# GpSimd's modulation slots through buffers and a queue of their own

## What is computed

```python
c_act = silu(c)
for layer in range(2):
    mod = c_act @ mod_w[layer] + mod_b[layer]
    sh1, sc1, g1, sh2, sc2, g2 = split(mod, 6)
    u = rms_norm(h, norm_mix[layer]) * (1 + sc1) + sh1
    mix = hgrn2_mixer(u, ...) if layer == 0 else chunk_band_attention(u, k_pad, v_pad, ...)
    h = h + g1 * mix
    u = rms_norm(h, norm_ffn[layer]) * (1 + sc2) + sh2
    h = h + g2 * swiglu(u, ffn_w_in[layer], ffn_w_out[layer])
    if layer == 0:
        k_pad, v_pad = shared_kv(h, c_act, kv_norm, kv_mod_w, kv_mod_b, kv_w)
```

## Time and profile before

| | |
|---|---|
| median of 3 runs | 2322.44 us (2321.78 to 2323.91) |
| the profiled execution | 2321.61 us |
| its span, first to last instruction | 2319.6 us |
| mean granted TensorE clock | 0.975 |
| TensorE busy | 2189.9 us (94%) |
| VectorE, ScalarE, GpSimd busy | 1410.4, 752.1, 424.3 us |
| GpSimd's multiply L593, 36 times | 3690 ns mean |
| GpSimd's first add L594, 36 times | 3473 ns mean |
| loads on SP into `raw` | 218 of 1024 KB, 4.8 us to landing |

### The profile page before, as it was taken

The page is one execution under the profiler, slowest core; times in us unless marked ns, Lnnn a source line. Parts: engine busy times, 40 slices in busy tenths (PEclk is TensorE's granted clock), DMA queues, the critical chain, the costliest instruction groups (busy, mean ns, idle before and its releaser), DMA issues.

```text
span 2319.6 us, 25720 instructions
## 1 busy us (share of the span) xinstructions
PE 2189.9 (94%) x10094; PEld 1752.1 (76%) x10094; DVE 1410.4 (61%) x1929; ACT 752.1 (32%) x961; POOL 424.3 (18%) x272
## 2 busy tenths in 40 slices
PE   7899999979999997999989999998999998999997
PEld 5588788767888886866678888876568876888885
DVE  5666766554767767177455444467565776655656
ACT  1443334332222223256432222244233333322321
POOL 0000000039998873200000000000420000000000
PEclk9999999989999998999999999999999998999998
DMA  6343231225555542422122322322112221323220
GB/s 245 124 161 109 92 127 57 71 84 188 200 182 182 182 163 94 143 91 74 52 76 91 99 101 91 109 94 69 41 48 98 92 81 65 109 91 109 91 91 37
DMA packets 39327, 249.54 MB, mean 108 GB/s; under 512 B 4627, under 2 KB 4819, under 8 KB 11112
## 3 DMA queue, kind: packets, MB, share of 16 engines
q1 hardware_dynamic: 32856, 230.97, 28.7%
q0 software_dynamic: 3008, 10.63, 1.4%
q10 hardware_dynamic: 3344, 6.29, 0.7%
HBM read 241.58 MB, written 6.29 MB: 107 GB/s over the span
## 4 chain that ended last, share of the span: by engine, by line
PE 81%; DVE 8%; issue 4%; POOL 3%; ACT 2%; DMA 1%; SPq 0%; ACTq 0%; DVEq 0%; POOLq 0%
PE bank L680 24%; PE bank L682 23%; PE bank L681 23%; PE bank L907 2%; DVE w_lo L1847 2%; PE bank L727 1%; ACT w_hi L1373 1%; PE bank L1025 1%; PE bank L1035 1%; PE bank L1046 1%; POOL raw L593 1%; PE bank L714 1%; DMA raw<-in_wts 1%; PE bank L823 1%; POOL raw L594 1%
## 5 line engine op out<-in xcount | busy, mean ns | idle before, releaser
L680 PE MATMUL bank<-u_hi,w_hi 128*128 128x512 f32 x1708 | 695.1, 407 | 40.3 <-DVE w_lo L1847 11.8
L682 PE MATMUL bank<-u_hi,w_lo 128*128 128x512 f32 x1708 | 672.9, 394 | 0.0
L681 PE MATMUL bank<-u_lo,w_hi 128*128 128x512 f32 x1708 | 672.8, 394 | 0.0
L1847 DVE TENSOR_TENSOR w_lo<-raw,w_hi 128x2048 fp32r<-128x2048 f32 x162 | 427.8, 2641 | 225.9 <-ACT w_hi L1373 225.8
L680 PEld LDWEIGHTS bank<-u_hi,w_hi 128*128 128x128 f32 x1708 | 325.8, 191 | 129.6 <-issue 49.0
L1373 ACT ACTIVATE w_hi<-raw 128x2048 fp32r<-128x2048 f32 x162 | 309.1, 1908 | 341.6 <-PE bank L682 300.4
L682 PEld LDWEIGHTS bank<-u_hi,w_lo 128*128 128x128 f32 x1708 | 325.0, 190 | 70.0
L681 PEld LDWEIGHTS bank<-u_lo,w_hi 128*128 128x128 f32 x1708 | 326.1, 191 | 67.0 <-issue 3.8
L680 PE MATMUL bank<-g_hi,w_hi 128*128 128x512 f32 x772 | 306.2, 397 | 13.8 <-DVE w_lo L1847 6.4
L681 PE MATMUL bank<-g_lo,w_hi 128*128 128x512 f32 x772 | 301.8, 391 | 0.0
L682 PE MATMUL bank<-g_hi,w_lo 128*128 128x512 f32 x772 | 301.7, 391 | 0.0
(11 more groups left out here) (284 smaller groups left out, 2262.0 us busy)
## 6 DMA issues: line engine op xcount, KB each, us to landing
raw<-in_wts SPq DMA_DIRECT2D x218, 1024.0 KB, 4.8
spectra<-pool ACTq DMA_DIRECT2D x16, 256.0 KB, 2.0
scr<-in_rel POOLq DMA_DIRECT2D x16, 256.0 KB, 3.4
pool<-spectra POOLq DMA_DIRECT2D x16, 256.0 KB, 3.0
H<-in_x ACTq DMA_DIRECT2D x1, 2048.0 KB, 21.3
out<-H SPq DMA_DIRECT2D x8, 256.0 KB, 2.0
pool<-in_window POOLq DMA_DIRECT2D x1, 1024.0 KB, 9.1
pool<-in_filt_w POOLq DMA_DIRECT2D x1, 512.0 KB, 6.2
```

Source lines behind the costliest of these rows:

```text
L680: pe.matmul(out, lh, rh, start=start, stop=False, skip_group_check=True)
L681: pe.matmul(out, lh, rl, start=False, stop=False, skip_group_check=True)
L682: return pe.matmul(out, ll, rh, start=False, stop=stop, skip_group_check=True)
L1847: dve.tensor_tensor(w_lo[RING[w]][:, :], raw[W_STREAM[w] % raw_ring][:, :], w_hi[RING[w]][:, :].bitcast(F32), ALU.subtract).then_inc(lo_do ...
```

## The change

M20 to M55 leave SyncE's list: its loop runs over `RING_ITEMS`, the weight slots and M0 to M19. The wait of an item for the one three places earlier stays, now among these. GpSimd loads its 36 slots itself, into three buffers `m_buf` in parts of `pool` that the FFN does not use, with a semaphore for each buffer. The first three loads are issued when TensorE has the first output of the mixer's output projection (wo0) ready. After the last add of slot m GpSimd waits for that add and issues the load of m + 3. The sums begin at the same place as before and are the same four instructions, in place, on the new buffers.

```diff
+RING_ITEMS = []
+_m = 0
+for _s in STREAM:
+    _m += _s[0] == "M"
+    if _s[0] == "W" or _m <= M_POOLED:
+        RING_ITEMS.append(_s)
+W_STREAM = [s for s, item in enumerate(RING_ITEMS) if item[0] == "W"]
+M_STREAM = [s for s, item in enumerate(RING_ITEMS) if item[0] == "M"]
...
+        m_buf = [pool[:, a:a + SLOT] for a in (4096, 6144, 12288)]
...
+        mod_in = [sem(f"mod_in{x}") for x in range(3)]
...
-            for s, item in enumerate(STREAM):
+            for s, item in enumerate(RING_ITEMS):
...
+            def load_mod(m):
+
+                i = m - M_POOLED
+                pl.dma_start(m_buf[i % 3], A["wts"][M_SOURCE + m]).then_inc(mod_in[i % 3], 16)
+
             def sum_mods():
 
+                pl.wait_ge(product, READY[FIRST["wo0"]])
+                for m in range(M_POOLED, M_POOLED + 3):
+                    load_mod(m)
                 pl.wait_ge(u_l, U_FFN0 + KC)
                 for m in range(M_POOLED, NM):
-                    s = M_STREAM[m]
-                    src = raw[s % raw_ring]
-                    pl.wait_ge(raw_in[s % raw_ring], 16 * (s // raw_ring + 1))
+                    i = m - M_POOLED
+                    src = m_buf[i % 3]
+                    pl.wait_ge(mod_in[i % 3], 16 * (i // 3 + 1))
...
                     pl.tensor_tensor(macc[:, m % MRING, :], src[:, 0:256], src[:, 256:512], ALU.add).then_inc(m_pooled, 1)
+                    if m + 3 < NM:
+                        pl.wait_ge(m_pooled, i + 1)
+                        load_mod(m + 3)
```

More of the change, by code:

```diff
@@ L154 @@
         M_BEFORE.append(len(W_LIST))
-W_STREAM = [s for s, item in enumerate(STREAM) if item[0] == "W"]
-M_STREAM = [s for s, item in enumerate(STREAM) if item[0] == "M"]
+RING_ITEMS = []
[6 more added lines that the diff above has]
+M_STREAM = [s for s, item in enumerate(RING_ITEMS) if item[0] == "M"]
 NW = len(W_LIST)
```

## The result

| | before | after |
|---|---|---|
| median of 20 runs each, same chip | 2322.44 us (2320.47 to 2330.74) | 2330.13 us (2323.15 to 2334.18) |
| ratio after / before | | 1.0027, 95% interval 1.0019 to 1.0035 |
| profiled execution | 2321.61 us | 2325.75 us |
| its span | 2319.6 us | 2323.9 us |
| mean granted TensorE clock | 0.975 | 0.972 |

The change makes the kernel slower, by 0.27% (6.3 us) on the ratio and 7.7 us between the medians. The forecast was 2321.0 and "no change"; the time lies inside the stated range, the direction does not.

A forecast was written before the change was run, and what follows sets the result against it. TensorE was taken to set the time (81% of the chain). Gains of 5.8 + 1.0 = 6.8 us less 6.3 in the norm leave 0.5: 2321.61 becomes 2321.1, stated as 2321; range 2317 to 2326, 8-in-10 range 2311 to 2335.

The forecast's parts named there:

- The wait moves from fi0_2's weights to M22's sum: Start of the first FFN: TensorE waits 5.4 us for M22, summed at 533.8, instead of 6.83 us for weights.
- FFN gain of 6.8 us: First FFN before fo0_10's low half: 5.8 us gained at its start plus 1.0 in the steady stretch.
- GpSimd's load issue, 0.65 us a slot: GpSimd in the FFN: each issue adds 0.65 us, giving 11.1 us a slot against TensorE's 11.52.
- the rival of a long issue: GpSimd's slots in the FFN: issue costs 1.4 us, slot 11.9, TensorE paced by sums, 2335 us in all; chance 0.15.
- The norm for the keys takes back 6.3: Norm before the keys: GpSimd's last sums slow VectorE's adds, costing 6.3 us of the 6.8 gained.
- mild rival: FFN and keys' norm: pace 11.4, no FFN wait, GpSimd at work until 908 over the diagonal; 2326 us, chance 0.10.
- Keys at 904.2: After the keys' norm: the key slots begin at 904.2 us instead of 904.72.
- 0.5 us is left, which nothing later changes: Behind the start of the keys: the remaining gain of 0.5 us stays unchanged to the end.
- All the signs that were to show the forecast wrong: GpSimd's sum-to-sum time outside 10.8 to 11.4, TensorE waiting for sums after 565 us, or keys'-norm adds of 0.68 us.
- The last addition: Whole kernel: 2321.1 us for the profiled execution, median of the runs 0.8 higher, stated as 2321.
- GpSimd early: FFN and keys' norm: pace 10.7, M52 summed at 853.8, 6 us gained, 2315.6 us; chance 0.23.
- all of it kept: FFN start: both waits and their cold stretches vanish, norm as before, 13.4 us gained, 2308.2 us; chance 0.05.

The follow-up runs named there:

- e7: e2 with M20 summed before GpSimd's wait for the FFN's input, during the output projection: 2307.19 us, ratio 0.9934.
- e8: e7 with the loads issued by SyncE in the old order of the stream: 2298.45 us, ratio 0.9909.
- e5: The changed kernel again, unaltered, one look for a third profile: 2332.29 us.
- e6: The changed kernel again, unaltered, one more look to catch an execution near 2330 us: 2330.44 us.
- e1: The changed kernel again, unaltered, for a second profile: 2328.13 us over 12 runs, ratio to before 1.0019.
- e3: The kernel before, with M52 to M55 held back until the keys' input is written: 2322.73 us, ratio 0.9996.
- e12: The kernel before, with VectorE building the keys' diagonal six times more than needed: 2327.82 us, ratio 1.0016.
- e4: The changed kernel with its three buffers, but SyncE issuing the loads in the old order of the stream: 2316.27 us, ratio 0.9978.
- e15: e8 without the early sum of M20, that is e2 with the loads on SyncE: 2307.20 us, ratio 0.9915.
- e2: The changed kernel, with M52 to M55 held back until the keys' input is written: 2310.10 us, ratio 0.9944.

## Why the prediction was wrong

Its steps, one by one:

- **The wait moves from fi0_2's weights to M22's sum.** Right. Forecast 5.4 us, measured 3.71 or 5.88. M22 was summed at 533.5 or 535.7, where I had 533.8, with 536 as a bound "where fo0_0's low half also gets in". That is just what happens, in the slow course. I gave one value, near the lower of two, and most executions take the other. e7 and e8 show that M20's sum done early removes the wait.
- **FFN gain of 6.8 us.** 11.4 in the fast course, 6.7 in the slow one. In the fast course both terms were too small: 7.9 us up to the end of fo0_0 (forecast 5.8) and some 3.9 in the steady stretch, where I had 1.0 and 2.3 at best. There TensorE needs 11.35 us a slot, with nothing left of the 0.17. (Both are taken at the modulation columns; fo0_10's `g_lo` takes 0.5 back.)
- **GpSimd's load issue, 0.65 us a slot.** Too low: 0.9 us (0.59 issue, 0.30 for its own add). The pace was 11.3 and 11.15 us where I had 11.1, so TensorE was still not held up, though barely at its 11.35; the rival of a long issue did not happen in the FFN. The transfers land in 5.3 us at the median, and I had priced them at 9.1; both are hidden.
- **The norm for the keys takes back 6.3.** Direction and mechanism right, price too low: 8.9 to 9.8 us (36.4 to 37.3 against 27.5). I had counted the adds, but fo0_10 itself is stretched as well (TensorE waits 2.99 us for `H` at 878.74): from its start to the column sums it is 26.2 and 28.1 us instead of 19.2. GpSimd was done at 901.1, over the building of the diagonal, as my mild rival had it (908).
- **Keys at 904.2.** Measured 903.88 and 904.73 in the fast course, 907.77 and 908.72 in the slow. Start to keys changed by -1.7 or +2.1 to +2.4 us.
- **"0.5 us is left, which nothing later changes".** This step failed. Behind the keys no instruction was altered, and the tail is 1.9 to 7.8 us longer in all four profiles of the changed kernel. What the runs show in its place: the same matmuls at a lower granted clock (over the tail 0.97 in after, 0.98 before), with waits of the same sum. Without it the fast course would have been as forecast, and the slow one 3 to 4 us slower, less than the 0.2%. All the signs that were to show the forecast wrong lie ahead of the keys, and none of them came up.
- **The last addition.** From 2321.1 for the profiled execution and 0.8 more for the median the sum is 2321.9, not 2321. It changes nothing here.

So the loss adds up as follows, against the span of before. Slow course (e5, e6): start to keys +2.1 and +2.2, tail +7.8 and +5.0, and 0.9 and 1.8 from a later start of the FFN (493.36 and 494.23 against 492.44) make the +10.9 and +9.0 of the spans. Fast course (after, e1): -1.7, tail +5.1 and +1.9, start +0.8 and +1.7: +4.3 and +1.9. The medians differ by 7.7 us, between the two. That most of the unprofiled runs take the slow course rests on the profiled ones' times (2323.3 and 2325.8 against 2330.4 and 2332.3) and on the two groups at clock 0.973; no profile of more of them shows it. That the fast course came out at the forecast's 904 us up to the keys is partly luck: the FFN gained 4.6 us more than forecast, and the norm took 3.5 more. The later start isn't explained. The changed kernel and its variants have 491.4 to 494.2, the kernel before 491.2 to 492.8, but with two lines that act only behind 850 us (e3, e12) it has 494.0 and 493.3; so the three early loads aren't needed for it.

Of the rivals, "GpSimd early" and "all of it kept" did not happen; e8 shows what the second needed (M20 early, the norm left free, the queue not on GpSimd), and up to the keys it gives more than the 13.4 us I had worked out: of the 24.4 us, 17.3 are the FFN's, 5.9 the norm's, whose own overlap went as well, and 1.1 an earlier start.

## What to carry to other kernels

Before work of a helper engine is moved forward, look where its tail then lands: here 36 slots moved to fill a stall, and the last four cost 14.9 us on the one short stretch where VectorE alone sets the time; a wait of two lines turned the loss into a gain. Give a background stream buffers of its own, and try its issues on an engine with nothing else to do: that was faster in each pair tried (e4 against e1, e8 against e7, e15 against e2), though up to the keys by 0.8 to 2.7 us only in the profiles. Where gain and loss are each under ten us, expect a result of a few us that the changed stage doesn't explain, and take several profiles of both kernels, from their slower executions too, before explaining one.

## What the hardware showed that I had not expected

- Issuing a 1024 KB load between two sums costs GpSimd 0.59 us and a 0.30 us wait for its own last write, 0.9 us in all; the transfer lands in 5.3 us at the median (5.0 to 10.5), against 4.9 on SyncE's queue.
- Two instructions that become ready within 0.02 us of each other, one on GpSimd and one on VectorE, come out in either order in different executions; 370 us later the kernel with the one order is 3.9 us ahead (903.88 against 907.77).
- Waits of 2 to 3 us are followed by a stretch at 1.2 GHz in one kernel and not in another: behind the same 2.17 us wait, identical work took 12.03 and 13.70 us. Over the last 1415 to 1423 us this alone makes 1.9 to 7.7 us, with the same 6162 matmuls and the same 49.3 to 49.6 us of waits.
- An operation on 128x8 elements takes 2.04 us of VectorE while GpSimd works on SBUF, and 0.17 us where GpSimd is idle (e2).
